# Feed-forward of a two-layer backbone: the residual rows stay on chip, gated blocks are added to them in place, and layer 1's rows are turned inside layer 0's last second product

## What is computed

```python
def trunk_layer(x, mod, p, ctx=None):
    sh1, sc1, g1, sh2, sc2, g2 = jnp.split(mod, 6, axis=-1)
    h = x * (1 + sc1) + sh1
    z = h @ w_in
    ...
    x = layer_norm(DEEPNORM_ALPHA * x + g1 * y, ln1_g, ln1_b)
    h2 = x * (1 + sc2) + sh2
    f = jnp.square(jax.nn.relu(h2 @ w_ff1)) @ w_ff2
    x = layer_norm(DEEPNORM_ALPHA * x + g2 * f, ln2_g, ln2_b)
```

## Time and profile before

| | us |
|---|---|
| median of 3 runs | 3282.41 |
| lowest, highest | 3281.67, 3282.5 |
| profiled execution, its own time | 3274.31 |
| span of the profiled execution | 3272.5 |
| granted clock over it | 0.971 of full |

### The profile page before, as it was taken

One profiled execution on the slowest core, in us unless ns is written; L12 is line 12 of the kernel. 1 busy time (PEld: TensorE's weight loads), 2 busy tenths in 40 slices (PEclk: granted clock), 3 DMA queues, 4 the chain that ended last, 5 costly groups with the idle time before them and its releaser, 6 DMA issues.

```text
span 3272.5 us, 44690 instructions
## 1 busy us (share of the span) xinstructions
PE 3081.0 (94%) x17016; PEld 2533.6 (77%) x17016; DVE 1657.3 (51%) x3082; ACT 983.9 (30%) x1904; POOL 429.1 (13%) x618
## 2 busy tenths in 40 slices
PE   5999989998999999999968999799989999999996
PEld 4788845567888888889848888455679998889995
DVE  4447677745533333333384376777456333333337
ACT  3222344536221122112233223445362221222221
POOL 0012333411000000000020022333110000000003
PEclk8999989999999999999989999899999999999999
DMA  5440210011422222220321102200112111111113
GB/s 216 158 134 24 75 70 0 0 68 52 131 76 78 84 77 78 77 89 26 125 94 37 44 25 76 77 0 0 56 58 90 52 39 39 52 39 39 52 33 148
DMA packets 99433, 220.10 MB, mean 67 GB/s; under 512 B 13392, under 2 KB 14000, under 8 KB 98736
## 3 DMA queue, kind: packets, MB, share of 16 engines
q1 hardware_dynamic: 78240, 151.76, 14.5%
q0 software_dynamic: 21008, 65.82, 5.5%
HBM read 191.01 MB, written 26.51 MB: 66 GB/s over the span
## 4 chain that ended last, share of the span: by engine, by line
PE 82%; DVE 6%; issue 3%; DMA 3%; ACT 2%; POOL 1%; ACTq 1%; DVEq 1%; POOLq 1%; SPq 0%
PE ps L1707 22%; PE ps L1711 21%; PE ps L1710 21%; PE ps L1922 6%; PE ps L1893 3%; PE ps L1912 2%; PE ps L1913 2%; PE ps L1689 2%; DVE nm L1448 1%; DMA w_raw<-in_w_slots 1%; PE ps L1820 1%; DVE w_lo L476 1%; DMA lnb<-in_ln_gb 1%; POOLq L554 1%; PE ps L1815 1%
## 5 line engine op out<-in xcount | busy, mean ns | idle before, releaser
L1707 PE MATMUL ps<-hi,w_hi 128*128 128x384 f32 x1584 | 540.0, 341 | 24.8 <-DVEq L414 17.7
L1711 PE MATMUL ps<-hi,w_lo 128*128 128x384 f32 x1584 | 533.4, 337 | 0.0
L1710 PE MATMUL ps<-lo,w_hi 128*128 128x384 f32 x1584 | 533.1, 337 | 0.0
L1707 PE MATMUL ps<-w_hi,f_hi 128*128 128x512 f32 x1152 | 457.2, 397 | 20.8 <-DVE acc L1606 20.8
L1710 PE MATMUL ps<-w_lo,f_hi 128*128 128x512 f32 x1152 | 450.5, 391 | 0.0
L1711 PE MATMUL ps<-w_hi,f_lo 128*128 128x512 f32 x1152 | 449.6, 390 | 0.0
L471 ACT CAST w_hi<-w_raw 128x512 fp32r<-128x512 f32 x368 | 214.1, 619 | 767.9 <-PE ps L1707 717.0
L1707 PE MATMUL ps<-w_hi,hi 128*128 128x512 f32 (+1 forms) x1008 | 388.2, 385 | 6.5 <-ACT stg L777 4.5
L1711 PE MATMUL ps<-w_hi,lo 128*128 128x512 f32 (+1 forms) x1008 | 380.2, 377 | 0.0
L1710 PE MATMUL ps<-w_lo,hi 128*128 128x512 f32 (+1 forms) x1008 | 379.8, 377 | 0.0
L1606 DVE TENSOR_TENSOR acc<-acc,ps 128x512 f32<-128x512 f32 x252 | 171.5, 686 | 359.6 <-PE ps L1711 359.4
(11 more groups left out here) (283 smaller groups left out, 4119.5 us busy)
## 6 DMA issues: line engine op xcount, KB each, us to landing
w_raw<-in_w_slots SPq DMA_DIRECT2D x368, 256.0 KB, 3.3
w_raw<-in_m_slots SPq DMA_DIRECT2D x160, 256.0 KB, 2.9
x_dram<-xr POOLq DMA_DIRECT2D x18, 512.0 KB, 3.3
x1t<-x_dram POOLq DMA_DIRECT2D x6, 1536.0 KB, 14.7
out<-acc POOLq DMA_DIRECT2D x18, 512.0 KB, 3.0
modw<-in_w_mod SPq DMA_DIRECT2D x4, 2048.0 KB, 16.1
acc<-in_x_in SPq DMA_DIRECT2D x3, 1536.0 KB, 23.0
zq_dram<-stg POOLq DMA_DIRECT2D x18, 256.0 KB, 2.4
```

The source lines that it names most:

```text
L1707: mm = pe.matmul(out, a_hi, b_hi, start=first, stop=False)
L1710: pe.matmul(out, a_hi, b_lo, start=False, stop=False)
L1711: return pe.matmul(out, a_lo, b_hi, start=False, stop=last)
```

## The change

Its parts:

- **Rows stay in `xr`.** `x1_dram`, `store1`, the loads of `x1t` and the order `X1_ORDER` go. `weighted1` writes alpha times the weighted rows (two SCALAR_TENSOR_TENSOR in place of two TENSOR_TENSOR).
- **`summed`** multiplies a block by the gate in place in PSUM and adds the result to the row half in `xr`: two instructions, with the row sum taken in the last chunk. The gate multiply and the alpha add per tile of 1,024 columns go. `gate2` has room of its own and is loaded after the first LayerNorm; the weights `lnb2` are loaded once `weighted1` is through.
- **`hidden`**: relu is written where `f_lo` will lie (`f_sq`), DVE squares it there and subtracts the rounded square in place. Since it squares in place, DVE starts only after ACT's rounded square. For the fourth 128 of a chunk's columns these places are the gaps between the row halves of `xr`.
- **Layer 0's end.** Its last second product also does what the first LayerNorm stage does: ACT normalises a tile (`normal1`), PE turns it (`next_turned`, eight transposes) two tiles behind the blocks, into banks 0, 1, 2, 6, and DVE and ACT apply the next layer's scale and shift, mixed with the LayerNorm weights, and write its `hi` and `lo` in place of `h2`. The rows themselves get their weights apart (`weighted2`) and are stored once all deviations are through.
- **No barrier** after layer 0, nor after the last layer. Waits in their place: PE and POOL wait for `f_acc`, each group of gate rows for `h_done` of its three tiles, `z_tile` for the stores that free `xr`, and ACT's move of the gate rows comes after `z_tile` 2 and waits for all nine rows (`y_rdy`). POOL issues layer 1's constants after the stores.

```diff
@@ pool, end of a layer @@
-                pool.wait_ge(S["h_ps"], START + 12 * NFF * (L + 1))
...
-                    pool.dma_start(x1t[:, 3 * u:3 * u + 3], x1_dram[3 * u:3 * u + 3].rearrange("t p d -> p t d")).then_inc(x1_ld[u], 16)
...
-                        deviation(2 * NT * L + NT + t, t, False)
-                    if t > 0:
+                        deviation(2 * NT * L + NT + t, t, L < NL - 1)
+                    if t > 0 and L == NL - 1:
                         store2(t - 1)
-                pool.wait_ge(S["ln_st"], 16 * NT * (L + 1))
-                phase(pool, L, 1)
+                for t in range(NT) if L < NL - 1 else ():
+                    store2(t)
@@ act @@
+            def modulated_next(L, t):
+                n, u = 2 * NT * (L + 1) + t, t % 2
+                act.wait_ge(S["xT_ps"], n + 1)
+                for kt in range(KT // 2, KT):
+                    act.activation(lo_row(t)[:, kt], ps[:, N_BANKS[u][1], (kt % 4) * P:(kt % 4 + 1) * P], ACT.Identity,
+                                   bias=mixed(0, kt, int(t < NS)), scale=mixed(1, kt, int(t < NS)))
+                act.drain()
+                act.wait_ge(S["hf_done"], START + n + 1)
+                act.copy(hi[:, :, t * P:(t + 1) * P], lo_row(t)).then_inc(S["hi_done"], 1)
...
+                    split_hi(act, L, 2 * NFF + 7, (S["f_ps"], START + 18 * NFF * (L + 1)), range(RAW))
+                    normal1(NT - 1, NT)
+                    modulated_next(L, 6)
+                    split_hi(act, L, 2 * NFF + 7, (S["f_ps"], START + 18 * NFF * (L + 1)), range(RAW, SLOTS))
+                    modulated_next(L, 7)
+                    modulated_next(L, 8)
@@ dve, summed @@
-                    a = acc[:, t, h_ * W:(h_ + 1) * W]
-                    if i:
-                        dve.tensor_tensor(a, a, ps[:, 3 + s_ % 3, :], ALU.add).then_inc(S["f_acc"], 1)
+                    a, f = x_half(t, h_), ps[:, 3 + s_ % 3, :]
+                    dve.tensor_tensor(f, f, gate2[:, int(t < NS), h_ * W:(h_ + 1) * W], ALU.mult)
+                    dve.drain()
+                    if i < NFF - 1:
+                        dve.tensor_tensor(a, a, f, ALU.add).then_inc(S["f_acc"], 1)
                     else:
-                        dve.tensor_copy(a, ps[:, 3 + s_ % 3, :]).then_inc(S["f_acc"], 1)
+                        dve.scalar_tensor_tensor(a, a, 1.0, f, ALU.mult, ALU.add, accum_out=mv[:, t, h_:h_ + 1]).then_inc(S["f_acc"], 1)
@@ pe, second_product @@
+                        if not by_halves and L < NL - 1 and t >= 2 and hf_:
+                            next_turned(t - 2)
@@ pe, start of a layer @@
-                for t in range(NT):
+                for t in range(NT) if not L else ():
...
-                phase(pe, L, 0)
+                if not L:
+                    phase(pe)
+                else:
+                    pe.wait_ge(S["f_acc"], START + 18 * NFF * L)
                 for g in range(3):
+                    if L:
+                        pe.wait_ge(S["h_done"], START + 2 * NT * L + 3 * g + 3)
```

More of the change, by code:

```diff
@@ L1620, in chunk @@
                         if not i:
[L1621 removed]
+                            weighted1(b)
                     split_lo(dve, L, 2 * i + 8, range(RAW))
@@ new lines, in _ @@
+                last = L == NL - 1
+                if not last:
+                    dve.drain()
+                    mixed_columns(lcol2, "lc2_ld", 0)
+                dve.wait_ge(S["ln_ld"], 32 * (L + 1))
+                for t in range(NT):
+                    for n in range(2):
+                        summed(NFF - 1, 2 * t + n, False)
+                    negated_mean(t, mv[:, t, 0:1], mv[:, t, 1:2])
+                    if last and t:
+                        normal(2 * NT * L + NT + t - 1, t - 1, x_row(t - 1), lnb2, S["y_rdy"])
+                    if not last and t >= 4:
+                        low_next(t - 4)
+                        weighted2(t - 4)
+                    if not last and t >= 3:
+                        modulate_next(t - 3)
@@ L1724, in _ @@
             for L in range(NL):
-                for t in range(NT):
+                for t in range(NT) if not L else ():
                     if t % 3 == 0:
                         pe.wait_ge(x_ld[t // 3], 16)
-                    if L or t > 2:
-                        pe.wait_ge(S["hi_done"], 2 * NT * L + t - 2)
+                    if t > 2:
+                        pe.wait_ge(S["hi_done"], t - 2)
                     for k in range(KT):
```

259 lines of the change are left out of this document (154 added, 105 removed).

## The result

The changed kernel takes 3238.48 us (median of 4, 3233.33 to 3242.9), the kernel before, run beside it, 3282.45 (3281.67 to 3284.77). The ratio is 0.9867, 95% interval 0.9855 to 0.988: 44 us faster, where 46 were forecast. The profiled execution took 3238.44, its span is 3236.2. The profiled execution of before lay 8 us under its kernel's median (3274.31, span 3272.5), so the two traces differ by 36.3 us, not by 44. Of the 37 executions of before on record (3274.08 to 3289.5) it is the second fastest, and no other has a granted clock on record above its 0.971. What follows compares traces, and splits the 36.3.

The account below looks back on a forecast made before the run. DVE was taken to bound both layer ends, PE the rest of the feed-forward. Gains of 33 (boundary) and 15.5 (layer 1's end) less 2.5 gave 46 us: 3228.3 profiled, 3236.4 us median, range 3226 to 3254.

Parts of the forecast that it names:

- The sum pair: DVE's gate product in PSUM plus add, per block: 0.76 + 0.70 = 1.46 us, with no surcharge for writing PSUM.
- The rival of the dear product: DVE's product written back into PSUM takes 1.23 us, the sum 2.0; 13 us off the gain, 3249 us; chance 10%.
- DVE bounds tiles 4 to 8: Layer 0's last second product: DVE needs 8.0 us a tile against PE's 6.36; tiles end from 1651.7 to 1684.1.
- Eight slots in 8.4 us: Layer 1's first eight weight slots at the boundary take 8.4 us, as in before, and end at 1694.6.
- boundary half lost: Stores issued when slots 4 to 7 are wanted, plus low PE clock, take 8 us off: 3244 us; chance 18%.
- The last remainder and the gate groups: Boundary: DVE's remainder 8 done at 1702.6, PE's third gate group at 1707.2, with 2 us taken off for low clock.
- What the missing barrier leaves: Start of layer 1: late stores and constants priced at nothing; `z_tile` 3 at 1721.3, PE needing the bank at 1721.6.
- Boundary, 33: Between the layers: third gate group 35.0 us earlier, less 2 for PE's low clock, gain 33 us.
- End of layer 1, 15.5: The 8.29 us `lnb2` wait goes, DVE tiles take 5.75 instead of 6.61 us; gain 15.5 us.
- Sums in ordinary products, nothing: The 14 ordinary second products: 194 us more DVE work costs nothing, hidden under PE's 2.72 us a block.
- Median, 8 above the profiled execution: Whole kernel: the forecast 3228.3 us for the profiled execution becomes 3236.4 for the median, 8 us above, as in before.
- The slower rival: A product so slow that DVE bounds the 14 ordinary products; decides from a 2.72 us sum, slower from 2.8; chance 2%.

## Why the prediction was right, point by point

To compare instants, 3.85 us are taken off the changed kernel's, its delay at the last hidden block.

- **The sum pair, 1.46 us.** 0.698 and 0.69, the second 0.76 behind: 1.45. No surcharge for writing PSUM. The rival of the dear product is out. The Trainium skill's figure for a PSUM source (VectorE: DVE Perf Modes, section on the TRN2 errata), 0.66, was lower than what was measured, as the row of the residual had said. (The 3 us that the prediction hung on it are too many by its own terms: 0.12 a tile, for five tiles and eight, is 1.6.)
- **DVE bounds tiles 4 to 8.** Tile 4's end was put at 1651.7 and came at 1651.6 (1655.44); tiles 7.92 apart, put at 8.1; tile 8's end 1683.3, put at 1684.1; remainder 5 at 1685.6, put at 1686.2. Each within 1 us.
- **Eight slots in 8.4 us: mis-sized.** They took 11.75, so the last ended at 1697.4, not 1694.6. That is the first half of the rival "boundary half lost", with its cause: the stores. It had 18%. Holding the stores gave 7.9. The Trainium skill, DMA: Bandwidth & Descriptors, section Queues, rings and completion order, has each DMA engine take turns among the queues packet by packet. I had read from it that the loads would be halved. In the direction that was right, and the forecast should have followed it at this one term, but the trace does not show even turns: of the engines' time the loads had 2.1% in the first 4 us and 26.6% in the next 3.
- **The last remainder and the gate groups.** 1705.7 and 1711.9 (the first z copy less one tile of 2.87), put at 1702.6 and, with the 2 us for the clock, 1709.2. 2.7 late, as the slots were. One step in the working was off without effect: the first group did not wait for slot 7, but began at 1696.03, before slot 4 was split (1697.06), and both groups were through 3.1 us before tile 8's remainder. So their half clock until 1700 cost nothing; the third group's, from 1710.6, cost 1.7 (5.8 in place of 4.15), and the 2 us set down for the clock were about right in size.
- **What the missing barrier leaves, priced at nothing.** Right. The constants are there at 1724.9, `z_tile` 3 is copied at 1728.6, and PE loses nothing that its waits show.
- **Boundary, 33.** 30.4; the 2.6 missing are the late slots.
- **End of layer 1, 15.5.** 17.0 from the last hidden remainder, of which 0.6 is that instant's own delay, so 16.4. Tiles 5.65 apart (put at 5.75); by the distance to the hidden remainder the last mean is at 3245.3 on before's clock, put at 3246.8; the tail behind it 10.2, put at 9.9.
- **Sums in ordinary products, nothing.** Right, and the cover was measured from both sides: nothing at 2.24, 58 us at 3.0 (2.92 from sum to sum).
- **Modulation rows, -2.5.** 2.2 measured (5.7 against 3.5).
- **Median, 8 above the profiled execution: not so for the changed kernel.** There the distance was zero, 3238.44 against 3238.48. By traces the sum was 46 and the result 36.3; by medians 44. What the traces lack is 7 us inside layer 1, most of it lower clock, 2.6 at the slots and 1.2 before any changed code (loads at the start), less 1.5 more at the end. The offset and the 7 us may be one thing: before's profiled execution was nearly its fastest, and if its usual one has that lower clock in layer 1, too, then to take 46 from the median was sound. They may also be two errors that stood against each other; then it is partly luck that the total came within 2 us. One trace of before cannot tell. The terms for the boundary and the end were right by themselves.
- **The slower rival.** Its mechanism is real (two more instructions made it so), and its price of 252 us for each us gives 50 at 2.92 from sum to sum, where 58 came; but its condition, a dear product, did not hold.

## What to carry to other kernels

A stretch where two engines hand tiles to each other can be forecast to a us or two from rows of similar instructions; what was priced too low is what enters the stretch from outside, here a burst of stores ahead of the loads that everybody waits for. Before making the engine that looks late faster, look in the order of the engine that waits: what stands ahead of the awaited instruction, and for what does that wait? And put a forecast on traces and on medians apart: one profiled execution can lie 8 us from its median, which is more than most single terms.

## What the runs showed of the hardware

- **GpSimd beside VectorE.** With GpSimd on `tensor_tensor` over SBUF, DVE's `tensor_tensor` with two SBUF inputs went from 1.22 to between 2.1 and 3.4 us (2.77 in the rows above), and from 0.62 to 2.77 for one weight slot of 512 elements (four in 2.49, then in 11.07). The short one takes as long as the long one, which fits that either waits for the end of an instruction of GpSimd's. The next four slots, beside which GpSimd paused for 2.3 us, took 4.67. With an input in PSUM, nothing changed.
- **Stores beside loads.** Five stores of 512 KB on GpSimd's queue, issued within 3.6 us, ahead of four loads of 256 KB on SyncE's: the DMA share was 0.92 at 310 GB/s from 1689 to 1701, where without them the loads had 0.50 at 146 GB/s from 1692 to 1700. The loads got 2.1% of the engines' time in the first 4 us and 26.6% in the next 3, and the slots came 3.9 us later.
- **An idle time of PE can be paid twice.** The 3.1 us wait that ended at 1709.6 cost another 1.7 at half clock behind it, and where it was removed the clock stayed up. The same wait of 2.7 us for `wt` was followed by different lengths of half clock in different traces.
